# Gates applied at the PSUM evacuation and expert outputs added to h inside eight accumulating gathers

## The reference, cut to what matters

```python
def second_block(x, ...):
    for l in range(DEPTH):                                  # 2 layers
        mix = token_mixing(x, ...)
        x = layer_norm_2(DN_ALPHA_2 * x + mix, ln1_g[l], ln1_b[l])
        ffn = moe(x, w_router, router_bias, w1[l], w3[l], w2[l])
        x = layer_norm_2(DN_ALPHA_2 * x + ffn, ln2_g[l], ln2_b[l])

# moe: every row goes to 2 of 16 experts (sigmoid scores, the best group of four);
# its two gates are the scores divided by their sum
    h = jax.nn.silu(xb @ w1[e]) * (xb @ w3[e])              # blocks of 128 rows of one expert
    yb = h @ w2[e]
    y = yb.reshape(-1, D) * slot_gate[:, None]
    return jnp.zeros((N + 1, D)).at[slot_tok].add(y)[:N]
```

## Time and profile before

| what | value |
|---|---|
| median of 3 runs | 3137.2 us (3133.65 to 3145.35) |
| the profiled execution | 3135.8 us, span 3133.5 us |
| TensorE busy | 2869.0 us, 92% |
| VectorE busy | 1796.9 us, 57% |
| ScalarE busy | 1431.0 us, 46% |
| GpSimd busy | 1089.4 us, 35% |
| mean granted clock of TensorE | 0.96 of full speed |
| moved by DMA | 468.87 MB, mean 150 GB/s |

### The profile page before, as it was taken

One profiled execution on the slowest core, in us unless ns is written; L12 is line 12 of the kernel. 1 busy time (PEld: TensorE's weight loads), 2 busy tenths in 40 slices (PEclk: granted clock), 3 DMA queues, 4 the chain that ended last, 5 costly groups with the idle time before them and its releaser, 6 DMA issues.

```text
span 3133.5 us, 45509 instructions
## 1 busy us (share of the span) xinstructions
PE 2869.0 (92%) x13536; PEld 2313.4 (74%) x13536; DVE 1796.9 (57%) x2649; ACT 1431.0 (46%) x2025; POOL 1089.4 (35%) x643
## 2 busy tenths in 40 slices
PE   6888999998889999999999978998599999969994
PEld 5666888886668888877877866887468777758883
DVE  4766434135684342157644158998557643279996
ACT  3525455226344553212445136887112453238884
POOL 2213344543214444645643521110356444501101
PEclk8999999999999999999999988999699999979997
DMA  4212233432113333534322348998334222449994
GB/s 125 61 34 88 81 97 97 154 110 71 48 41 102 99 94 122 168 95 108 101 72 58 104 151 297 411 411 331 119 95 114 79 61 75 153 162 410 411 411 164
DMA packets 379302, 468.87 MB, mean 150 GB/s; under 512 B 35122, under 2 KB 281988, under 8 KB 379076
## 3 DMA queue, kind: packets, MB, share of 16 engines
q1 hardware_dynamic: 353664, 392.05, 37.3%
q0 software_dynamic: 14688, 53.48, 4.4%
q10 hardware_dynamic: 10724, 20.65, 2.2%
HBM read 423.62 MB, written 35.65 MB: 147 GB/s over the span
## 4 chain that ended last, share of the span: by engine, by line
PE 48%; issue 33%; POOL 12%; DVE 3%; ACT 2%; DMA 2%; ACTq 1%; POOLq 0%; SPq 0%; DVEq 0%
POOL unit_lo L411 10%; PE bank L491 7%; PE bank L492 6%; PE bank L2059 4%; PE bank L2201 4%; PE bank L2205 4%; PE bank L2202 4%; PE bank L806 2%; PE bank L2215 2%; PE bank L2219 2%; PE bank L2216 2%; PE bank L906 1%; PE bank L909 1%; PE bank L907 1%; PE bank L2132 1%
## 5 line engine op out<-in xcount | busy, mean ns | idle before, releaser
L411 POOL TENSOR_TENSOR unit_lo<-unit_raw,unit_hi 128x1024 fp32r<-128x1024 f32 (+2 forms) x194 | 465.3, 2401 | 862.0 <-ACT unit_hi L404 862.0
L491 PE MATMUL bank<-xT_hi,unit_hi 128*128 128x512 f32 (+1 forms) x1776 | 694.0, 394 | 10.8 <-DVE d_lo L2663 3.8
L492 PE MATMUL bank<-xT_lo,unit_hi 128*128 128x512 f32 (+1 forms) x1776 | 671.1, 381 | 0.0
L491 PEld LDWEIGHTS bank<-xT_hi,unit_hi 128*128 128x128 f32 x1776 | 339.1, 191 | 99.0 <-issue 29.7
L492 PEld LDWEIGHTS bank<-xT_lo,unit_hi 128*128 128x128 f32 x1776 | 339.5, 191 | 64.9 <-issue 6.1
L404 ACT ACTIVATE unit_hi<-unit_raw 128x1024 fp32r<-128x1024 f32 (+2 forms) x194 | 203.0, 1047 | 380.4 <-PE bank L806 152.7
L396 POOL TENSOR_TENSOR unit_lo<-unit_raw,unit_hi 128x1024 fp32r<-128x1024 f32 (+3 forms) x154 | 317.7, 2063 | 12.8
L394 POOL TENSOR_SCALAR unit_hi<-unit_raw 128x1024 fp32r<-128x1024 f32 (+3 forms) x154 | 145.6, 946 | 474.7 <-PE bank L2059 267.5
L476 DVE TENSOR_TENSOR wt_lo<-wt,wt_hi 128x1024 fp32r<-128x1024 f32 x192 | 229.0, 1221 | 28.8 <-ACT wt_hi L471 27.8
L476 DVE TENSOR_TENSOR xT_lo<-wt,xT_hi 128x1024 fp32r<-128x1024 f32 x192 | 234.4, 1223 | 12.8 <-ACT xT_hi L471 2.9
L806 PE MATMUL bank<-xT_hi,unit_lo 128*128 128x512 f32 x976 | 241.1, 389 | 0.0
(11 more groups left out here) (523 smaller groups left out, 6186.8 us busy)
## 6 DMA issues: line engine op xcount, KB each, us to landing
wt<-in_w SPq DMA_DIRECT2D x384, 512.0 KB, 8.2
unit_raw<-in_w_in SPq DMA_DIRECT2D x276, 256.0 KB, 3.1
unit_raw<-in_w_ffn_up SPq DMA_DIRECT2D x176, 256.0 KB, 3.1
unit_raw<-in_w_ffn_down SPq DMA_DIRECT2D x88, 256.0 KB, 3.1
unit_raw<-in_w_out SPq DMA_DIRECT2D x64, 256.0 KB, 2.9
y_rows<-yb POOLq DMA_DIRECT2D x30, 512.0 KB, 7.2
y_rows<-zeros POOLq DMA_DIRECT2D x24, 512.0 KB, 5.2
unit_raw<-in_w_br SPq DMA_DIRECT2D x96, 128.0 KB, 2.3
```

The source lines that it names most:

```text
L411: pool.eng.tensor_tensor(lo, raw, hi.bitcast(F32), SUB).then_inc(self.split, 1)
L491: pe.matmul(out, wh, xh, start=first, stop=False)
L492: pe.matmul(out, wh, xl, start=False, stop=False)
```

## The change

- **Gates at the evacuation.** VectorE multiplies `slot_d` by the gates and splits the result into a high and a low part (`slot_gh`, `slot_gl`). TensorE turns both, in 16 more small products with `slot_p`, into `sgate`, the gate behind every place of every block. They stand in TensorE's program behind the transposes of the first expert's rows. VectorE copies the result out of PSUM between `x_low(0)` and the third unit's low part. ScalarE uses the column of expert e as the scale when it brings the result out of PSUM, and the loop for extra blocks does the same on VectorE. What lies in `y_rows` is then multiplied already.
- **Alpha times h.** GpSimd multiplies the four tiles of h by alpha in place, one beside each of the experts 1 to 4, behind the store of the expert before.
- **The sums.** The eight gathers have `h` as their destination and add in the transfer (`compute_op=ADD`). Their order is `ADD_ORDER`. The second gather into a tile waits until the first has landed. `rows_scaled`, `yg` and the two additions of `experts_added` are gone, and VectorE waits for both gathers of a tile.
- **The root's table.** ScalarE takes the root of a constant when it has issued the last store, ahead of the layer norm.

```diff
 # splits2 (GpSimd), in the loop over experts
                 if e:
                     store(e - 1)
+                if 0 < e <= NT:
+                    g.tensor_scalar(h[:, e - 1, :], h[:, e - 1, :], ALPHA, 0.0, MUL, ADD).then_inc(h_scaled.sem, h_scaled.up(G))
...
             G.eng.wait_ge(y_last.sem, G.alone(y_last.at(G, 2)))
-            for n in range(2 * NT):
+            G.eng.wait_ge(h_scaled.sem, G.alone(h_scaled.last(G)))
+            for a, i in ADD_ORDER:
+                if a:
+                    G.eng.wait_ge(ygl[i].sem, G.alone(ygl[i].at(G, 1)))
                 g.indirect_dma_start(
-                    out=yg[n], out_offset=None, in_=y_dram,
-                    in_offset=bass.IndirectOffsetOnAxis(ap=desti[:, n % 2, n // 2:n // 2 + 1], axis=0)).then_inc(ygl[n // 2].sem, ygl[n // 2].up(G))
+                    out=h[:, i, :], out_offset=None, in_=y_dram,
+                    in_offset=bass.IndirectOffsetOnAxis(ap=desti[:, a, i:i + 1], axis=0), compute_op=ADD).then_inc(ygl[i].sem, ygl[i].up(G))
+        ADD_ORDER = ((0, 0), (0, 1), (0, 2), (1, 0), (1, 1), (0, 3), (1, 2), (1, 3))
...
 # tensor2
             x_turned(0)
+            T.eng.wait_ge(slot_oh.sem, slot_oh.at(T, 2))
+            for part in (slot_gh, slot_gl):
+                for n in range(2 * NT):
+                    last = pe.matmul(bank[7][:, 0:NB + 2], slot_p[:, n, :], part[:, n, :], start=part is slot_gh and n == 0, stop=part is slot_gl and n == 2 * NT - 1)
+            last.then_inc(rt_mm.sem, rt_mm.up(T))
...
 # scalar2
+                    if e == 0:
+                        A.eng.wait_ge(rt_dest.sem, rt_dest.at(A, 2))
                     for x in range(2):
                         c = slice(x * S, x * S + S)
-                        act.activation(yb[e % 2][:, c], bank[5 + x][:], ACT.Copy).then_inc(y_ev.sem, y_ev.up(A))
+                        act.activation(yb[e % 2][:, c], bank[5 + x][:], ACT.Copy, scale=sgate[:, e:e + 1]).then_inc(y_ev.sem, y_ev.up(A))
...
-            def rows_scaled(i):
-                A.eng.wait_ge(ygl[i].sem, A.alone(ygl[i].at(A, 2)))
-                act.activation(yg[2 * i], yg[2 * i], ACT.Identity, scale=gw[:, i, 0:1]).then_inc(yg_sc.sem, yg_sc.up(A))
-
-            norm_a(A, 1, False, rows_scaled)
+            act.activation(sd[:, 0:1], eps, ACT.Sqrt).then_inc(a_step.sem, a_step.up(A))
+            A.eng.wait_ge(a_step.sem, A.alone(a_step.last(A)))
+            norm_a(A, 1, False)
...
 # vector2, behind the gates gw
+            for a in range(2):
+                c = slice(NT * a, NT * a + NT)
+                v.tensor_tensor(slot_d[:, c, :], slot_d[:, c, :], over(gw[:, :, a:a + 1], [P, NT, NB + 2]), MUL).then_inc(v_step.sem, v_step.up(V))
+            V.eng.wait_ge(v_step.sem, v_step.last(V))
+            v.tensor_copy(slot_gh[:], slot_d[:]).then_inc(v_step.sem, v_step.up(V))
+            V.eng.wait_ge(v_step.sem, v_step.last(V))
+            v.tensor_tensor(slot_gl[:], slot_d[:], slot_gh[:].bitcast(F32), SUB).then_inc(slot_oh.sem, slot_oh.up(V))
...
             x_low(0)
+            V.eng.wait_ge(rt_mm.sem, rt_mm.at(V, 4))
+            v.tensor_copy(sgate[:], bank[7][:, 0:NB + 2]).then_inc(rt_dest.sem, rt_dest.up(V))
             for n in range(2, Feed.SPLIT):
...
             def experts_added(i):
-                a, b = yg[2 * i], yg[2 * i + 1]
-                V.eng.wait_ge(yg_sc.sem, yg_sc.at(V, i + 1))
-                v.scalar_tensor_tensor(a, b, gw[:, i, 1:2], a, MUL, ADD).then_inc(yg_use.sem, yg_use.up(V))
-                V.eng.wait_ge(yg_use.sem, yg_use.last(V))
-                v.scalar_tensor_tensor(h[:, i, :], h[:, i, :], ALPHA, a, MUL, ADD).then_inc(yg_use.sem, yg_use.up(V))
-                V.eng.wait_ge(yg_use.sem, yg_use.last(V))
+                V.eng.wait_ge(ygl[i].sem, V.alone(ygl[i].at(V, 2)))
```

More of the change, by code:

```diff
@@ L116 @@
     "y_last": (0, 0, 2),
-    "yg_sc": (0, 0, 4),
+    "h_scaled": (0, 0, 4),
     "yg_ld0": (0, 0, 2),
@@ L149 @@
     "a_ot": (0, 0, 4),
-    "rt_mm": (0, 0, 3),
+    "rt_mm": (0, 0, 4),
     "gb_ld": (2, 4, 4),
@@ L157 @@
     "la_part": (0, 4, 0),
-    "a_step": (0, 11, 0),
+    "a_step": (0, 11, 1),
     "gv_ev": (0, 8, 4),
@@ L191 @@
     "gt_use": (0, 0, 26),
-    "v_step": (24, 237, 339),
+    "v_step": (24, 237, 342),
     "norm_var": (4, 8, 8),
@@ L231 @@
     "be_ok": (0, 0, 1),
-    "slot_oh": (0, 0, 1),
-    "rt_dest": (0, 0, 1),
+    "slot_oh": (0, 0, 2),
+    "rt_dest": (0, 0, 2),
     "x_lo": (0, 0, 33),
@@ L236 @@
     "h_lo": (0, 0, 17),
-    "yg_use": (0, 0, 8),
 }
@@ L718, in norm_v, with norm_a @@
             low(NT - 1)
-        def norm_a(A, n, held=True, rows_scaled=None, beside=None):
+        def norm_a(A, n, held=True, beside=None):
             def deviation(i):
@@ L1715, in build @@
                       for w, x in ((wt_hi, xT_hi), (wt_lo, xT_lo))))
-        yg = [wt[:, i, :] for i in range(2 * NT)]
         rsc, rbi = s7("rsc", [P, NT, NE]), s7("rbi", [P, NT, NE])
@@ L1720, in build @@
         slot_ge, slot_d = (s7(n, [P, 2 * NT, w]) for n, w in (("slot_ge", NB + 3), ("slot_d", NB + 2)))
-        slot_b, slot_p = (s7(n, [P, 2 * NT, w], F32R) for n, w in (("slot_b", NB + 2), ("slot_p", P)))
+        slot_b, slot_p, slot_gh, slot_gl = (s7(n, [P, 2 * NT, w], F32R) for n, w in (("slot_b", NB + 2), ("slot_p", P), ("slot_gh", NB + 2), ("slot_gl", NB + 2)))
+        sgate = s7("sgate", [P, NB + 2])
         hot2, d128 = s7("hot2", [P, NT, NE]), s7("d128", [P, 2 * NT])
@@ L1763, in build @@
             "gt_sig", "gt_use", "mg_hi", "mg_lo", "rt_sc", "rt_oh", "rt_mm", "rt_dest", "be_ok", "slot_oh"))
-        x_tr, x_hi, x_lo, act_h, h_val, h_tr, h_hi, h_lo, y_ev, yg_use = (signal(n) for n in (
-            "x_tr", "x_hi", "x_lo", "act_h", "h_val", "h_tr", "h_hi", "h_lo", "y_ev", "yg_use"))
+        x_tr, x_hi, x_lo, act_h, h_val, h_tr, h_hi, h_lo, y_ev = (signal(n) for n in (
+            "x_tr", "x_hi", "x_lo", "act_h", "h_val", "h_tr", "h_hi", "h_lo", "y_ev"))
         ov_begin, ov_products, ov_read, ov_val = (signal(n) for n in ("ov_begin", "ov_products", "ov_read", "ov_val"))
@@ L1774, in build @@
         PAR2 = 9
-        xb_ld, y_st, y_last, yg_sc = signal("xb_ld", 16), signal("y_st", 16), signal("y_last", 16), signal("yg_sc")
+        xb_ld, y_st, y_last, h_scaled = signal("xb_ld", 16), signal("y_st", 16), signal("y_last", 16), signal("h_scaled")
         ygl = [signal(f"yg_ld{i}", 16) for i in range(NT)]
@@ L2837, in vector2 @@
                     for x in range(2):
[L2838 removed]
+                        v.tensor_scalar(yb[0][:, x * S:x * S + S], bank[5 + x][:], flat(sgate[:].rearrange("p (n a) -> p n a", a=1)[:, bass.ds(bb + NE, 1), :]), None, MUL).then_inc(ov_val.sem, ov_val.up(V))
                 V.loop_end(NOV)
             def experts_added(i):
[L2842 to L2847 removed]
+                V.eng.wait_ge(ygl[i].sem, V.alone(ygl[i].at(V, 2)))
             norm_v(V, 1, None, experts_added)
```

7 lines of the change are left out of this document (removed).

## The result

The changed kernel takes 3150.01 us (median of 18 runs, 3141.75 to 3156.68), the kernel before 3139.23 us (18 runs beside it, 3133.65 to 3145.74). The ratio is 1.0036, with a 95% interval of 1.0029 to 1.0044: 10.8 us slower. That is inside the range and within 0.5%, but the interval lies clear of 1, on the other side of it than the 3136 of the forecast. The profiled execution has a span of 3148.3 us, 14.8 more than before.

The account below looks back on a forecast made before the run. It took TensorE to bound the experts and VectorE the tail. Tail -1.4 and start +1.1, over two layers, gave -0.6: 3135.2 us profiled, 3136 as the median, range 3120 to 3158.

Parts of the forecast that it names:

- The tail: Behind the experts' products: VectorE's adds and ScalarE's scalings go, adding gathers take r = 2.76 us each; gain 1.4 us a layer.
- Rival 1: Gathers in the tail: adding is free, r = 1.45, 7.0 us gained a layer, 3125 (3122 with early clock); chance 0.24.
- rival 2: Gathers in the tail: adds starve their queue; 3159 at three times the plain price, 3193 at r = 6.8; chance 0.13.
- The start: Before the experts: 16 small products delay the first up product; +1.1 us a layer, between -0.4 and +2.3.
- The routing: VectorE's added gate operations in the routing, about 1.3 us, hidden by 2.68 us of idle time.
- The scalings: GpSimd's four scalings of h beside experts 1 to 4: taken as 0, ends 0 and 4.5 us a layer.
- The evacuation: ScalarE's evacuation with the gate: a scaled copy replaces a copy of the same shape, cost 0.
- Rival 3: Experts and start: GpSimd's scalings and the late first product cost their full bounds, +10.8 us, 3148; chance 0.10.

Follow-up runs that it names:

- The plain gathers: Kernel after with the same eight gathers and waits, but plain into the free weight buffer, so expert rows are not added to h: 3138.79 us in one run.
- Version 2: Version 1 with three of eight gathers adding in the transfer, the others plain and added by VectorE, no waits between gathers: 3134.97 us, 0.9984.
- Version 1: Kernel after with 12 filler transposes, h scaled on VectorE behind the last expert, and the 16 products ahead of the first transposes: 3138.6 us, 0.9993.
- The scale alone: Kernel before with only a column of ones as the scale of ScalarE's evacuation: 3143.86 us, 1.0010.
- the multiplications alone: Kernel before with four GpSimd multiplications of h by 1.0 where the change puts the scalings: 3146.6 us, 1.0020.

## Why the prediction was right and wrong

**The tail: right.** I took r = 2.76 us for an adding gather, and 2.72 was measured; the wait for the seventh was to come at about 23 us and came at 22.75; the gain was to be 1.4 us and is 1.7 here, 1.3 by the means of all profiles. The 1.45 of a plain gather was a busy time of the DMA engines, and 2.72 is a spacing of landings. Like with like, the spacings are 2.73 against 1.58 us, a ratio of 1.7. The busy times are 2.95 against 1.46 us, a ratio of 2.0 (the gathers' queue is busy 82.6% of 3107.4 to 3136 us, and 68.7% of 3091 to 3108 before). The Trainium skill, page "Collectives: The Full Stack", section "The bandwidth ceiling: the fold count and why AG != RS != AR", has 1.93 for a reducing transfer; the trace agrees in size. Rival 1 (free) and rival 2 (starved) both fall. The plain gathers show what rival 1 would have been worth: 6.8 us a layer more than the change. One detail was missed: issuing an adding gather costs GpSimd 1.6 us and not 1. Issues stand 1.9 us apart where nothing else holds them, under the 2.7 of the landings, so the transfers still set the pace.

**The first layer's share of it: only partly found.** The next layer's first product comes 1.35 us sooner after the first gather (40.49 for 41.84 us), but at the wait some 110 us in, 0.6 is left (109.4 for 110.0), and at the next gather of rows it is 0.35 later than before. That difference says little. The whole stretch takes 594.7 to 595.4 us in the four profiles with the old tail, and 594.5 to 595.7 in the five with the new one. Version 2 had 2.8 us at that first product, 2.0 at 110 us and 0.6 at the gather. A large gain does arrive: with the plain gathers it is 7.0 us at 110 us and 6.3 at the gather. GpSimd's last gather comes at 21.8 us instead of 8.8, and its weight splits behind it; the prediction left them where they were. Where the rest of version 2's gain goes was not settled.

**The start: right.** I said +1.1 a layer, with the clock rising at the same moment; it was +0.8 and +1.1, and the clock rose within 0.3 us of that moment. The five profiled kernels with the products at this place take 38.7 to 39.0 us up to the first store. The six with them elsewhere or without them take 37.7 to 38.1. Version 1, which moves the products, gets the first layer's back whole and most of the second's.

**The routing: right.** VectorE's operations for the gates lie behind the issue of the first gather of rows. They take up 1.5 of the 2.68 us in which VectorE idled ahead of the rows' low part, and 1.21 are left.

**The scalings: wrong.** The step that failed is "I take 0: it idles 20 of 260 us, and four units of split weights lie between it and TensorE". The measured cost is 2.3 and 1.9 us a layer, about half of the end of 4.5 that stood beside it. TensorE's waits on hs beside the scalings are the sign that the prediction had named for this. The units buffer the weights, but VectorE also makes hs, which TensorE turns at once, and hs queues behind the splits. The right question was what else stands in that queue, and the one wait on hs of 0.5 us in the kernel before showed that the path had little slack. The page that I cited against the edit was right: the Trainium skill, "SBUF — State Buffer", section "Who interferes with whom". The trace agrees with it, with 3.66 us instead of 2.36 for two splits beside one scaling of 1.06. I found the rule and its row and let a mean idle time outweigh both. By the rule alone, with the rest of the sum, I'd have said 3145.6.

**The evacuation: wrong.** The step is "replaces a copy by a scaled copy of the same shape: 0". It is 0.69 us instead of 0.60. By itself this gives 0.2 us in the experts and 0.3 in the gap. The clock's fall gives 2.5 a layer and was in no case of mine. It came with 0.18 us more idle time at a place where little was missing for it. The scale alone brought the fall in one layer of two, and the scalings alone in both, so the fall isn't shown to be the scale's alone; that filled idle time prevents it is shown. No row of mine looked at the stretch between the last expert's up products and the gather of y.

**Rival 3** came out at its 10.8 us by accident. Half of its price for the scalings is there and less than half of its price for the start; the clock makes up the sum.

In us over both layers, from the one pair of profiles: scalings +4.2, half clock +5.0, evacuations +1.1, start +1.9, tail -1.7, the first layer's tail and what follows it +0.35. That is 10.85, against the 10.8 of the medians. The first three were predicted as nothing.

**Open:** why the multiplications alone lowered the clock at 1.76 us in both layers, when four other layers at 1.76 kept it. The timelines of that place show the same instructions with the same idle times. Theory and rival both fall in their pure form: idle time of 1.61 us was safe and 1.94 mostly not, and at 1.76 something else has a say. The traces do show that the moment of the fall moves between executions with the same instructions. In five layers (the kernel after, the plain gathers, the scale alone) it came 0.1 to 0.7 us after the start of the last transposes of hs and cost 2.5 us. In four (the scalings left out, the multiplications alone) it came 1.6 to 2.6 us after it, and half clock lasted half as long and cost 1.5 to 1.7 us. No run controlled this moment, so it stays a rival to the length of the idle time. More executions of each weren't tried.

## What to carry to other kernels

When an engine has slack on average, list what each instruction on it feeds before you give it more work: a queue can hold a buffered product and an unbuffered one, and the unbuffered one has the slack that counts. Price a scaled copy by a row of its own, and look at what 0.1 us does to idle times of TensorE near which its clock has fallen; a few useless transposes are a cheap guard, worth 5 us here. An adding gather is no free add: with landings 2.7 us apart against 1.6 it pays where the engine's add stands in the path, and not for the rows that start the chain, so mix the two.

## What was not expected of the hardware

- With 1.94 us of idle time ahead of four transposes on TensorE, and 1.41 behind them, the granted clock fell from 1.00 to 0.50 in 7 of 8 layers, with 1.76 in 2 of 6; in the changed kernel this lasted some 7 us and cost 2.5 us. 12 or 3 transposes of 128x128 (1.47 or 0.49 us) in that idle time kept it at 1.00 in all 8.
- ScalarE's copy of 128x512 from PSUM takes 0.69 us with a scale from a column and 0.60 without.
- Accumulating gathers of 512 KB into SBUF land 2.73 us apart where plain ones land 1.58 apart, and the issue of one holds GpSimd for 1.54 to 1.64 us instead of 0.94 to 0.98.
- One GpSimd scaling of 128x1024 (1.06 us) made two VectorE splits beside it take 3.66 us instead of 2.36.
